# Joining the two halves of each fill slab in the RWKV iterations of a hybrid decoder step

## The reference

```python
h = _rmsnorm(x, norm1_g) * (1 + scale1) + shift1      # scale, shift, gate: silu(c) @ w_ada
z = h @ w_in                                          # RWKV columns, q, k, v, two branch gates
o_a = (rwkv7(z[:, :Z_A]) * g) @ w_proj_a              # 16 heads of 64
o_b = moba(rope(q), rope(k), v, paged cache) @ w_proj_b
x = x + gate1 * ((sigmoid(gate_a) * o_a + sigmoid(gate_b) * o_b) @ w_out)
# then: adaLN RMSNorm, up-projection, causal convolution, GELU, gate, down-projection, final RMSNorm
# rwkv7, per head and token:
s = s * w_t - (s @ kk_t) (kk_t * a_t) + v_t k_t;   y_t = s @ r_t
```

## Time and profile before

| | us |
|---|---|
| median of 3 runs (lowest, highest) | 2472.8 (2471.74, 2476.32) |
| profiled execution: its own time, its span | 2472.71, 2470.8 |
| TensorE busy, weight loads | 2342.4, 2056.3 |
| DVE, ACT, POOL busy | 1111.0, 954.9, 105.3 |
| mean granted clock of TensorE | 0.968 of 2.4 GHz |
| stretch of the eight RWKV iterations in the span | 313 to 1098 |

### The profile page before, as it was taken

How to read it: one execution, slowest core, us unless ns; L and a number is a source line. 1 busy time by engine, 2 the same in 40 slices (tenths; PEclk the granted TensorE clock), 3 DMA queues, 4 the chain that set the end, 5 groups by cost and what they waited for, 6 DMA issues and landing times. The chain is left out here.

```text
span 2470.8 us, 49844 instructions
## 1 busy us (share of the span) xinstructions
PE 2342.4 (95%) x19856; PEld 2056.3 (83%) x19856; DVE 1111.0 (45%) x1757; ACT 954.9 (39%) x1391; POOL 105.3 (4%) x224
## 2 busy tenths in 40 slices
PE   6899999999999999988998999799999999999998
PEld 2399977878878788655665999699999999999998
DVE  1343445354453544434433554555545445544433
ACT  1133334343343433325343333245545455433333
POOL 0000010000000100100000000000101000000000
PEclk7999999999999999969898999899999999999999
DMA  9955455665656656566887445255555555555543
GB/s 307 349 165 162 134 167 184 191 189 177 192 184 185 184 177 191 187 215 208 305 322 282 154 154 165 91 163 168 162 166 165 163 168 162 168 165 162 162 147 120
DMA packets 322267, 461.06 MB, mean 187 GB/s; under 512 B 37073, under 2 KB 203747, under 8 KB 321635
## 3 DMA queue, kind: packets, MB, share of 16 engines
q1 hardware_dynamic: 314477, 450.39, 57.5%
q10 hardware_dynamic: 7634, 8.38, 1.0%
HBM read 442.83 MB, written 15.86 MB: 186 GB/s over the span
## 5 line engine op out<-in xcount | busy, mean ns | idle before, releaser
L910 ACT ACTIVATE whi<-raw 128x1024 fp32r<-128x1024 f32 x496 | 524.8, 1058 | 887.5 <-PE ps L1874 861.5
L1874 PE MATMUL ps<-hhi,whi 128*128 128x288 f32 x2752 | 834.1, 303 | 15.4 <-DVE hlo L1404 12.6
L1874 PE MATMUL ps<-hhi,wlo 128*128 128x288 f32 x2752 | 812.5, 295 | 0.0
L1874 PE MATMUL ps<-hlo,whi 128*128 128x288 f32 x2752 | 811.9, 295 | 0.0
L1360 DVE TENSOR_TENSOR wlo<-raw,whi 128x1024 fp32r<-128x1024 f32 x384 | 469.9, 1225 | 653.7 <-ACT whi L910 653.6
L1874 PEld LDWEIGHTS ps<-hhi,whi 128*128 128x128 f32 x2752 | 517.7, 188 | 60.4 <-issue 39.8
L1874 PEld LDWEIGHTS ps<-hlo,whi 128*128 128x128 f32 x2752 | 518.0, 188 | 1.2
L1874 PEld LDWEIGHTS ps<-hhi,wlo 128*128 128x128 f32 x2752 | 517.6, 188 | 0.0
L1874 PE MATMUL ps<-fhi,whi 128*128 128x288 f32 x704 | 208.0, 295 | 2.8 <-DVE wlo L1360 2.8
L1874 PE MATMUL ps<-fhi,wlo 128*128 128x288 f32 x704 | 207.7, 295 | 0.0
L1874 PE MATMUL ps<-flo,whi 128*128 128x288 f32 x704 | 207.3, 294 | 0.0
(11 more groups left out here) (374 smaller groups left out, 2697.1 us busy)
## 6 DMA issues: line engine op xcount, KB each, us to landing
raw<-in_w_up SPq DMA_DIRECT2D x352, 256.0 KB, 2.9
raw<-in_w_in SPq DMA_DIRECT2D x160, 512.0 KB, 4.0
raw<-in_w_ada SPq DMA_DIRECT2D x128, 512.0 KB, 4.7
raw<-in_w_down SPq DMA_DIRECT2D x88, 512.0 KB, 3.8
kpage<-in_w_ada SPq DMA_DIRECT2D x64, 512.0 KB, 7.2
kpage<-in_cache_k SPq DMA_DIRECT2D x64, 512.0 KB, 5.4
kpage<-in_cache_v SPq DMA_DIRECT2D x64, 512.0 KB, 5.3
raw<-in_w_out SPq DMA_DIRECT2D x32, 512.0 KB, 3.8
```

The costliest lines, as they stand in the source:

```text
L910: return act.activation(o, i, ACT.Copy, **k)
L1874: return pe.matmul(out, lhsT, rhs, start=start, stop=stop, **k)
```

## The change

`fill(i, 0)` does nothing any more, and `fill(i, 1)` issues both halves, with the first half's waits, at the place of the second half. ACT, DVE, POOL and SP keep their orders.

```diff
             def rwkv(j, dense):
 
                 def fill(i, half):
-                    if dense:
-                        rest(j, i, half)
+                    if dense and half:
+                        rest(j, i, 0)
+                        rest(j, i, 1)
```

## The result

The changed kernel takes 2510.7 us, the median of four runs (2506.4 to 2514.8), against 2474.6 for the kernel before on the same chip (2471.7 to 2481.4): 1.0139 times as long, 95% interval 1.0118 to 1.0159, or +34 us (29 to 39); the two medians are 36 apart. The forecast was +26.9, the range ended at +39.

The account below looks back on a forecast made before the run. TensorE itself was taken to bound the kernel, busy 99.75 of 102 us. Terms summed to +4.57 us an iteration, 32.0 in seven, less 5.1 at the turns: +26.9 on 2472.7, forecast 2499.6, range 2484 to 2512.

Parts of the forecast that it names:

- 1a to 3a, adaLN slab: First-half places of slabs 1 to 3: TensorE waits longer for ada(j, 1)'s second slab, whose landing stays; +1.60 us an iteration.
- 4a: First-half place of slab 4, covering POOL's masks for level 0: bare wait 0.94 us, net +0.82 an iteration.
- 5a: First-half place of slab 5, covering ACT's copies of Xs and Xss: bare wait 0.57 us, net +0.46 an iteration.
- 6a, 7a, 8a: First-half places of slabs 6 to 8, covering DVE's level subtraction: no idle expected, -0.10 us each, -0.30 an iteration.
- 9a: First-half place of slab 9: ACT's copy of Xs comes late, queued behind slab 10's cast; net +0.83 us an iteration.
- 10a, 12a: First-half places of slabs 10 and 12, covering s0T and DVE's Ublk: results ready, -0.19 us each an iteration.
- 11a: First-half place of slab 11: ACT's copy Mss stands behind slab 12's cast; net +0.22 us an iteration.
- 14a: First-half place of slab 14, covering two DVE operations between gn_means and gn_vars; net +1.32 us an iteration.
- turn, six times: Turn between iterations: TensorE's wait of 0.85 us for v_sq goes, six times, -5.1 in all.
- The rival that the slab isn't pinned: The adaLN slab's transfer lands earlier, so its term is 0 and 11.2 us go: 2488.4 us; chance 0.13.
- clock rival: TensorE's clock falls behind longer waits, chiefly at the adaLN slab: 8 to 23 us more, 2508 to 2523; chance 0.11.
- Drains only: Results are ready anyway, so 11 places gain at most 0.19 us each: faster, 2453.0 us; chance 0.04.

Follow-up runs that it names:

- e1: The kernel before with only slabs 1, 2 and 3 joined: 1.0062 of the kernel before, +15 us.
- e5: The changed kernel with slab 2 moved ahead of ada(j, 1), over the adaLN slab's wait: 1.0068 of the kernel before, +17 us.
- e8: The changed kernel run once more, unaltered, its profile being the second one: 1.0157 of the kernel before, +39 us.
- e3: The kernel before with only slabs 6, 7, 8, 10 and 12 joined: 0.9989 of the kernel before, -3 us.
- e4: The changed kernel with slabs 9 and 11 left in halves: 1.0116 of the kernel before, +29 us.
- e11: The changed kernel with slab 2 ahead of ada(j, 1) and slabs 9 and 11 in halves: 1.0028 of the kernel before, +7 us.

## Why the prediction was right

Term by term, per iteration, from the starts of the same instructions in the first profile of the change:

| term | forecast | measured |
|---|---|---|
| 1a to 3a, adaLN slab | +1.60 | +1.33 |
| 4a | +0.82 | +0.82 |
| 5a | +0.46 | +0.44 |
| 6a, 7a, 8a | -0.30 | -0.27 |
| 9a | +0.83 | +0.88 |
| 10a, 12a | -0.38 | -0.38 |
| 11a | +0.22 | +0.26 |
| 14a | +1.32 | +1.31 |
| turn, six times | -0.85 | -0.91 |

**The mechanism was the forecast one.** The passes are work and cover at once: at the ready places only the drain was saved, at 4a, 5a, 9a, 11a and 14a the time saved up to the wait was less than the 1.60 that the same passes cost later. ACT's copies behind the two casts were read rightly; in the fourth iteration they came as the sum had them:

```profile
695.36 0.38 ACT L910 ACTIVATE Xs<-ps 64x256 f32<-64x256 f32 x1
...
708.22 0.25 ACT L910 ACTIVATE Mss<-ps 32x128 f32<-32x128 f32 x1
```

**The adaLN term was too large by 0.27.** The slab is pinned as said: in all seven iterations, before and after, its matmul starts 0.04 us behind the landing. The transfer took less, on average 4.90 us from issue to landing where it was 5.16 before; in the fourth iteration it was issued at 645.38, 4.75 ahead of its use at 650.13:

```profile
645.38 0.38 SPq L643 DMA_DIRECT2D raw<-in_w_ada  x1
```

The prediction let the landing stay to the hundredth and took the iteration with the longest wait for its example; the average of the waits of before was half of that the earlier trace rows, and the longest of after is 2.5 us where the prediction had 3.3. This is 1.9 us in seven. The rival that the slab isn't pinned is excluded by e1 and e5.

**The clock was left out of the sum.** It stood as a rival of 8 to 23 us with 0.11, and with the sign that the granted clock would be visibly below 1. It is: 0.99 and 0.98 over the dense iterations of the two profiles. The sum as it came out, with the terms above, is 25.3; with 0.6 more at place 13b, where two iterations waited 0.28 for the slab of `ada(j, 7)`, and 6.1 of half clock it is 32.0, against 31.7 measured. The second profile has 10.7 of half clock. So both cases came true together: the forecast's waits in full, and of the rival some 6 to 11 us, in the second profile alone at the place it named (the adaLN slab) and in both at places it did not (9a, once 11a). Its price was too high: it put 3.29 us on a place, for a whole group of 24 at half clock, while each stretch of the first profile lasted 3.41 us, slowed some 14 of the 24 passes and cost 1.53. The argument that the other stretches keep long groups of 24 was no protection: the fall came inside such a group, which followed the small matmuls and the wait. The Trainium skill (TensorE: Matmul & The Clock Gate, Part 1) says that the clock follows how busy TensorE has recently been, and that the number of slow matmuls at a kernel's start varies from run to run. Inside this kernel it varied too, with four stretches in one profile and seven in the other.

**How near it was.** The 2510.7 us lie 1.3 us inside the end of the range and also within the clock rival's 2508 to 2523; e8's 2515.4 lie beyond the range. The waits were forecast, but that the range held with the clock left out of the sum is in part luck.

**Drains only** was excluded by all five bare places, each at its price. e3 shows how little that rival had to offer where it does hold: 0.09 to 0.19 us a place.

## What to carry to other kernels

Filler work between dependent steps is priced by the wait that it hides and not by its own length: for each place compare the bare wait with the drain, and join only where the wait is nil. When filler is moved onto another wait, look at what the step behind it releases on the queues: here state stores, issued behind a waiting transfer, took back what the cover had gained, and the gain came only with the stores moved as well. A bare wait among small matmuls should be given a price for the clock too, as a sum over the places where it may fall.

## What the runs showed of the hardware that was not expected

The granted clock fell to 0.50 behind a stretch in which TensorE was busy 2.35 of 3.36 us, with one wait of 1.01 us in it, and in e3 behind one in which the trace has it busy for all of 3.41 us, with no fill pass begun. A stretch of 3.41 us at half clock over fill passes cost 1.53 us, half as much again as that wait. Which of several such places is hit differed between two executions of the same kernel, and taking one kind of place away moved the fall to another (e4); with both kinds gone there was none in the one profile of e11.
